# Five norms made as a row: two rounded products with a tile of 1/1024, root and reciprocal of the whole row

## The chip, the cores and the metric

The kernel runs on one core of one Trainium2 chip. The metric is the time on the device in microseconds (us), as the median of several runs.

## The reference

Two transformer blocks of width 1024 over 512 tokens, all in fp32. Cut to the order of work and the norms of the change:

```python
def rms_norm(x, w):                                    # over the 1024 channels of a token
    return x * rsqrt(mean(x * x, axis=-1) + 1e-6) * w

# first block
x = x + 0.5 * swiglu(rms_norm(x, norm_ffn1_w), w_in, w_out)        # n_ffn1
x = x + hybrid_mixer(rms_norm(x, norm_mix_w), ...)                 # n_mix
x = x + memory_cross_attention(rms_norm(x, norm_cross_w), ...)     # n_cross
x = x + 0.5 * swiglu(rms_norm(x, norm_ffn2_w), w_in, w_out)        # n_ffn2
x = rms_norm(x, norm_final_w)                                      # n_fin
# second block
...
x = x + rms_norm(mixed, g_post_mix)                                # n_post0, n_post1 (halves)
f = square(relu(rms_norm(x, g_pre_mlp) @ w_up)) @ w_down           # n_mlp
x = x + rms_norm(f, g_post_mlp)                                    # n_pmlp0, n_pmlp1 (halves)
x = x + sigmoid(rms_norm(x, g_ple) @ w_ple_gate) * (p @ w_proj)    # n_ple
```

## The kernel before

**Layout.** Activations lie transposed: channels on the 128 partitions in 8 chunks, the 512 tokens along a row. A weight unit is 128x1024 and gives one output tile of 128 channels by 512 tokens in 8 chunks. Every matrix product is made of three fp32r products (`products`, L510 on): rounded weight by rounded operand (L516), rounded weight by the operand's rest (L517), the weight's rest by the rounded operand (L518). The rounding is `w_hi` and `w_lo` for weights, `gx_hi` and `gx_lo` for the operand. A tile is 24 products.

**The stream of weights.** The 364 units go through a ring of four: SyncE loads `w_raw`, ScalarE casts it to `w_hi` (L1283), GpSimd subtracts to `w_lo` in four quarters (L463), TensorE uses it. ScalarE's casts stand in its program between its other work (`ahead`), three units ahead of use, and each waits until TensorE is done with the unit that had the slot.

**The norms.** The factor of a token isn't applied to the operand but to the result of the product, as a row `rstd_row` that all partitions hold (for instance L1851, which makes `ff_gate` from a bank and the row and thereby frees the bank). So TensorE starts on the first tiles of a stage before the factor is known, and it stops where all banks of the stage are full: `tiles` waits for `tile_free` of the bank's last use. The factor is made beside the first tiles, with two hooks that `norm_hooks` gives and that stand at fixed chunks in TensorE's stream:

1. `stat` (L700): the squares of the 8 chunks are already added up in `sumsq` (or `post_sum`, which is `rfin_row`). Four fp32 products of each 128 columns with a column of ones put the sums of 128 tokens each in a column of bank 7.
2. ScalarE takes the root of the 128x4 column with scale 1/1024 (L1296), VectorE its reciprocal (L1782).
3. `row` (L707): four transposes turn the column, broadcast over 128 partitions, into the 128x512 row in bank 7. VectorE copies it to `rstd_row` (L1786), and its next instruction uses it.

Where the hooks stand: in both feed-forward stages the first three tiles are made together; `stat` comes behind them, `row` behind chunk 3 of the fourth tile. For n_cross they stand behind the first tile of `cq` and behind chunk 3 of the second. For n_mlp they stand behind chunks 1 and 7 of a half tile in `tail_of_group`. For n_ple `stat` stands in `gate(3)`, and `row` between `project(0)` and `project(1)`; the second half of `project(1)` writes a bank that VectorE's first `gate` has to free.

**What sets the order.** All orders are written out by hand, one instruction stream for an engine, with semaphores between them. Each norm has a count on the semaphores `norm_stat`, `norm_root`, `norm_col`, `norm_row` and `norm_ready`, which `norm_count` computes.

## Time and profile before

| | |
|---|---|
| median of 3 runs | 2134.77 us (2134.74 to 2136.09) |
| span of the profiled execution | 2133.4 us |
| TensorE busy | 2114.8 us, 99% |
| VectorE, ScalarE, GpSimd busy | 829.8, 803.6, 1120.5 us |
| longest groups | the three products of `gx`, 675, 668 and 668 us |

The median of the runs is 1.4 us above the span, which runs from the first to the last instruction of the profiled execution. In the rows, PE is TensorE's products, PEld its weight loads, DVE VectorE, ACT ScalarE, POOL GpSimd. An arrow in brackets says who ended the idle time that stood before an instruction.

### The profile page before, as it was taken

What the parts mean: (1) busy time and instruction counts of PE and PEld (TensorE: products, weight loads), DVE (VectorE), ACT (ScalarE), POOL (GpSimd) and SP (SyncE); (2) the same over time, 40 slices, a digit from 0 to 9 for tenths busy, and PEclk for the clock granted to TensorE, in tenths of its full rate; (3) what the DMA queues carried; (4) which work ended last, traced back from release to release, by engine and by line L of the source; (5) the groups of instructions that cost most, each with busy time, mean ns of one, the idle gap of its engine ahead of it and who ended that gap; (6) DMA issues with size and microseconds to landing.
All of it is one profiled execution on the core that took longest, in us unless ns stands there. A gap on an engine that the chain in (4) does not pass through costs nothing.

```text
span 2133.4 us, 29164 instructions
## 1 busy us (share of the span) xinstructions
PE 2114.8 (99%) x10122; PEld 1740.7 (82%) x10122; DVE 829.8 (39%) x1489; ACT 803.6 (38%) x1345; POOL 1120.5 (53%) x1493
## 2 busy tenths in 40 slices
PE   9999999999999999999999999999999999999999
PEld 7888888878887778877888888887787888888887
DVE  5222211762841766143322222208744474023244
ACT  5222232325834655323322223326554343122233
POOL 6555555673354337725655555554545466555554
PEclk9999999999999999999999999999999999999999
DMA  6322233233322213412332223321222223332322
GB/s 214 119 98 98 99 106 106 85 99 96 114 99 79 75 55 122 155 40 89 99 98 98 95 94 117 99 96 63 79 89 79 89 80 108 99 99 99 99 89 80
DMA packets 61344, 207.71 MB, mean 97 GB/s; under 512 B 6616, under 2 KB 8088, under 8 KB 61256
## 3 DMA queue, kind: packets, MB, share of 16 engines
q1 hardware_dynamic: 55216, 195.84, 27.8%
q10 hardware_dynamic: 6040, 10.65, 1.5%
q8 instruction: 61, 1.00, 0.2%
q14 instruction: 27, 0.22, 0.0%
HBM read 204.31 MB, written 4.77 MB: 98 GB/s over the span
## 4 chain that ended last, share of the span: by engine, by line
PE 42%; issue 28%; POOL 27%; DVE 2%; POOLq 0%; ACT 0%; DMA 0%; SPq 0%; DVEq 0%; ACTq 0%
POOL w_lo L463 27%; PE bank L516 11%; PE bank L518 11%; PE bank L517 11%; PE bank L678 1%; PE bank L680 1%; PE bank L679 1%; PE bank L908 1%; PE bank L932 1%; PE bank L840 1%; PE bank L920 0%; DVE gx_lo L2394 0%; DVE bank L2403 0%; PE bank L846 0%; DVE x L2405 0%
## 5 line engine op out<-in xcount | busy, mean ns | idle before, releaser
L463 POOL TENSOR_TENSOR w_lo<-w_raw,w_hi 128x256 fp32r<-128x256 f32 x1448 | 1087.1, 783 | 933.4 <-ACT w_hi L1283 933.3
L516 PE MATMUL bank<-gx_hi,w_hi 128*128 128x512 f32 (+1 forms) x1768 | 674.9, 382 | 7.8 <-DVE gx_lo L2394 4.5
L518 PE MATMUL bank<-gx_hi,w_lo 128*128 128x512 f32 (+1 forms) x1768 | 668.1, 378 | 0.0
L517 PE MATMUL bank<-gx_lo,w_hi 128*128 128x512 f32 (+1 forms) x1768 | 667.6, 378 | 0.0
L1283 ACT CAST w_hi<-w_raw 128x1024 fp32r<-128x1024 f32 x364 | 378.4, 1045 | 347.9 <-PE bank L518 291.8
L516 PEld LDWEIGHTS bank<-gx_hi,w_hi 128*128 128x128 f32 x1768 | 332.6, 188 | 74.2 <-DVE gx_lo L2394 6.4
L518 PEld LDWEIGHTS bank<-gx_hi,w_lo 128*128 128x128 f32 x1768 | 332.5, 188 | 62.1
L517 PEld LDWEIGHTS bank<-gx_lo,w_hi 128*128 128x128 f32 x1768 | 332.7, 188 | 60.5 <-issue 0.2
L516 PE MATMUL bank<-ff_hi,w_hi 128*128 128x512 f32 x352 | 136.9, 389 | 0.0
L517 PE MATMUL bank<-ff_lo,w_hi 128*128 128x512 f32 x352 | 136.9, 389 | 0.0
L518 PE MATMUL bank<-ff_hi,w_lo 128*128 128x512 f32 x352 | 136.9, 389 | 0.0
L516 PE MATMUL bank<-up_hi,w_hi 128*128 128x512 f32 (+1 forms) x288 | 105.4, 366 | 0.0
L517 PE MATMUL bank<-up_lo,w_hi 128*128 128x512 f32 (+1 forms) x288 | 105.3, 365 | 0.0
L518 PE MATMUL bank<-up_hi,w_lo 128*128 128x512 f32 (+1 forms) x288 | 105.3, 365 | 0.0
L1854 DVE TENSOR_TENSOR ff_up<-bank,rstd_row 128x512 f32<-128x512 f32 x44 | 30.4, 690 | 189.9 <-PE bank L518 189.9
L1355 ACT CAST ff_hi<-ff_act 128x512 f32 (+1 forms) x44 | 27.3, 620 | 188.8 <-DVE ff_act L1858 188.8
L518 PEld LDWEIGHTS bank<-ff_hi,w_lo 128*128 128x128 f32 x352 | 66.1, 188 | 13.8
L516 PEld LDWEIGHTS bank<-ff_hi,w_hi 128*128 128x128 f32 x352 | 66.1, 188 | 13.7
L517 PEld LDWEIGHTS bank<-ff_lo,w_hi 128*128 128x128 f32 x352 | 66.1, 188 | 13.6
L1351 ACT ACTIVATE ff_silu<-ff_gate 128x512 f32<-128x512 f32 x44 | 27.8, 632 | 119.7 <-DVE ff_gate L1851 119.7
L1851 DVE TENSOR_TENSOR ff_gate<-bank,rstd_row 128x512 f32<-128x512 f32 x44 | 30.4, 691 | 90.7 <-PE bank L518 90.6
L678 PE MATMUL bank<-w_hi,gx_hi 128*128 128x512 f32 x160 | 63.7, 398 | 0.4 <-ACT z_tok L1337 0.4
(358 smaller groups left out, 2703.4 us busy)
## 6 DMA issues: line engine op xcount, KB each, us to landing
w_raw<-wstream SPq DMA_DIRECT2D x364, 512.0 KB, 3.5
bias_spread<-bias_rows ACTq DMA_DIRECT2D x1, 2560.0 KB
square<-cum_rows ACTq DMA_DIRECT2D x8, 256.0 KB, 3.5
rfin_row<-cum_rows ACTq DMA_DIRECT2D x8, 256.0 KB, 3.1
outT<-ple_o SPq DMA_DIRECT2D x8, 256.0 KB, 2.0
x<-xT SPq DMA_DIRECT2D x3, 512.0 KB, 8.0
square<-bias_spread ACTq DMA_DIRECT2D x4, 256.0 KB, 2.6
rfin_row<-bias_spread ACTq DMA_DIRECT2D x4, 256.0 KB, 2.7
```

The source lines that it names most:

```text
L463: ins = nc.gpsimd.tensor_tensor(w_lo[:, s, part], w_raw[:, s, part], w_hi[:, s, part].bitcast(F32), ALU.subtract)
L516: nc.tensor.matmul(dst, hi, rhs[0], start=first, stop=False)
L517: nc.tensor.matmul(dst, hi, rhs[1], start=False, stop=False)
L518: return nc.tensor.matmul(dst, lo, rhs[0], start=False, stop=last)
L678: nc.tensor.matmul(dst, a[0], rh, start=(k == 0), stop=False, skip_group_check=True)
L679: nc.tensor.matmul(dst, a[1], rh, start=False, stop=False, skip_group_check=True)
L680: mm = nc.tensor.matmul(dst, a[0], rl, start=False, stop=(k == DC - 1), skip_group_check=True)
L1283: nc.scalar.copy(w_hi[:, j, :], w_raw[:, j, :]).then_inc(unit_hi, 1)
L1351: nc.scalar.activation(ff_silu[:, :], ff_gate[:, :], ACT.Silu).then_inc(sem("ffn_silu"), 1)
L1355: nc.scalar.copy(tile_of(ff_hi, c), ff_act[:, :]).then_inc(sem("ffn_act_hi"), 1)
L1851: nc.vector.tensor_tensor(ff_gate[:, :], bank[2 * j][:, :], rstd_row[:, :], ALU.mult)\
L1854: nc.vector.tensor_tensor(ff_up[:, :], bank[2 * j + 1][:, :], rstd_row[:, :], ALU.mult)\
```

## The change

For n_ffn1, n_cross, n_ffn2, n_mlp and n_ple the column is gone. ScalarE rounds the sum row to `sum_hi` (`high_sum`), VectorE makes the rest `sum_lo` (`row_norm`), and one hook, `row_mean`, at the place of the old `row`, makes two fp32r products of 512 columns with a 128x128 tile `mean_r` of 1/1024. That sums over the partitions and puts the mean on all of them at once. ScalarE then takes the root of the 128x512 row from PSUM to `rstd_row` (`root_row`), and VectorE the reciprocal of that row in place. The other norms stay. The code for the new waits: ScalarE's two casts of weights now stand between `high_sum` and `root_row` in the feed-forward stages, one cast stands between them at n_cross, none at n_mlp, two at n_ple. `mean_r` is made once at the start, ahead of the small cast `wdt_hi`. Three tiles find their place in 15 KB that a smaller DMA scratch leaves; `x`, `cols` and `wdt` start 128 bytes lower, everything behind them where it was. Two semaphores for late loads become one, and `setup_hi` takes the place of `wdt_hi`.

```diff
+ROW_NORMS = ["n_ffn1", "n_cross", "n_ffn2", "n_mlp", "n_ple"]
...
+        sum_hi = fixed("sum_hi", [S], F32R)
+        sum_lo = fixed("sum_lo", [S], F32R)
+        mean_r = fixed("mean_r", [P], F32R)
+        assert cursor[0] <= 16384
+        cursor[0] = 16384
         x = fixed("x", [DC, S])
...
+            def row_mean(name):
+
+                def mean():
+                    if name == "n_ffn1":
+                        pe.wait_ge(sem("setup_hi"), 1)
+                    pe.wait_ge(norm_sem("col"), norm_count("col", name, 1))
+                    nc.tensor.matmul(bank[7][:, :], mean_r[:, :], sum_hi[:, :], start=True, stop=False)
+                    nc.tensor.matmul(bank[7][:, :], mean_r[:, :], sum_lo[:, :], start=False, stop=True)\
+                      .then_inc(norm_sem("row"), 1)
+                return mean
...
                 tiles(f"{name}_in", gx, DC, 4, peel=1, ready=gx_ready(before),
-                      hooks=norm_hooks(norm, before, together=3) + hooks, banks=4, together=3, opening=opening)
+                      hooks=(((3, 3), row_mean(norm)),) + hooks, banks=4, together=3, opening=opening)
...
-            (_, stat), (_, row) = norm_hooks("n_cross", "mix_attn")
-            one_tile("cq", 0, range(DC), gx, ready=gx_ready("mix_attn"), then={7: stat})
-            one_tile("cq", 1, range(DC), gx, then={3: row})
+            one_tile("cq", 0, range(DC), gx, ready=gx_ready("mix_attn"))
+            one_tile("cq", 1, range(DC), gx, then={3: row_mean("n_cross")})
...
-            (_, stat), (_, row) = norm_hooks("n_mlp", "post")
-            tail_of_group("up_a", {1: stat, 7: row})
+            tail_of_group("up_a", {7: row_mean("n_mlp")})
...
-            gate(3, {1: stat})
+            gate(3)
             project(0)
-            row()
+            row_mean("n_ple")()
             project(1)
...
+            def high_sum(name, summed):
+
+                if summed in POSTS:
+                    act.wait_ge(sem("post_summed"), post_count(summed, 2 * DC))
+                else:
+                    act.wait_ge(sem("summed"), sum_count(summed, DC + 1))
+                wait(act, norm_sem("row"), norm_count("row", name, 0))
+                nc.scalar.copy(sum_hi[:, :], (post_sum if summed in POSTS else sumsq)[:, :]).then_inc(sem("sum_hi"), 1)
+
+            def root_row(name):
+
+                act.wait_ge(norm_sem("row"), norm_count("row", name, 1))
+                nc.scalar.activation(rstd_row[:, :], bank[7][:, :], ACT.Sqrt, bias=eps_col[:, :], scale=1.0)\
+                  .then_inc(norm_sem("root"), 1)
...
                         if first(i) and j == 0:
-                            norm(norm_name)
+                            high_sum(norm_name, before)
                             for uu in (1, 2):
                                 ahead(f"{name}_in", i, 4, uu)
+                            root_row(norm_name)
...
+            nc.scalar.activation(mean_r[:, :], ones, ACT.Copy, scale=1.0 / D).then_inc(sem("setup_hi"), 1)
+            nc.scalar.copy(wdt_hi[:, :, :], wdt[:, :, :]).then_inc(sem("setup_hi"), 1)
...
+            def row_norm(name, summed):
+
+                src = post_sum if summed in POSTS else sumsq
+                if summed in POSTS:
+                    dve.wait_ge(sem("post_summed"), post_count(summed, 2 * DC))
+                dve.wait_ge(sem("sum_hi"), ROW_NORMS.index(name) + 1)
+                nc.vector.tensor_tensor(sum_lo[:, :], src[:, :], sum_hi[:, :].bitcast(F32), ALU.subtract)\
+                  .then_inc(norm_sem("col"), 1)
+                dve.wait_ge(norm_sem("root"), norm_count("root", name, 1))
+                nc.vector.reciprocal(rstd_row[:, :], rstd_row[:, :])\
+                  .then_inc(norm_sem("ready"), 1)
+                dve.wait_ge(norm_sem("ready"), norm_count("ready", name, 1))
...
-    nc = bacc.Bacc("TRN2", target_bir_lowering=False, num_devices=1)
+    nc = bacc.Bacc("TRN2", target_bir_lowering=False, num_devices=1, dynamic_dma_scratch_size=1024)
```

TensorE's rows at n_ffn2 before, from the last products of the third tile (bank 2) over the fourth (bank 3) to the row's block and beyond. `consts` holds the ones and the identity.

```order
L517 MATMUL bank2<-gx_lo_54,w_hi_56 128x512
L518 MATMUL bank2<-gx_hi_53,w_lo_57 128x512
L700 MATMUL bank7<-consts_58,sumsq_61 128x1 x4
L516 MATMUL bank3<-gx_hi_53,w_hi_56 128x512
...
L518 MATMUL bank3<-gx_hi_53,w_lo_57 128x512
L707 MATMUL bank7<-consts_58,rstd_col_70 128x128 x4
L516 MATMUL bank3<-gx_hi_53,w_hi_56 128x512
L517 MATMUL bank3<-gx_lo_54,w_hi_56 128x512
```

The same place of the change (L524 to L526 are the three products there):

```order
L525 MATMUL bank2<-gx_lo_57,w_hi_59 128x512
L526 MATMUL bank2<-gx_hi_56,w_lo_60 128x512
L524 MATMUL bank3<-gx_hi_56,w_hi_59 128x512
...
L526 MATMUL bank3<-gx_hi_56,w_lo_60 128x512
L726 MATMUL bank7<-sum_hi_49,mean_r_51 128x512
L727 MATMUL bank7<-sum_lo_50,mean_r_51 128x512
L524 MATMUL bank3<-gx_hi_56,w_hi_59 128x512
```

The block behind the third tile is gone, and the block behind twelve products of the fourth is two products of 512 columns.

ScalarE's rows at the same norm before, from the end of stage `co` on:

```order
L1308 ACTIVATE square<-x 128x512
L1283 CAST w_hi<-w_raw 128x1024
L1296 ACT_TABLE_LOAD
L1296 ACTIVATE root_col<-bank,eps_col 128x4
L1283 CAST w_hi<-w_raw 128x1024 x2
L1351 ACT_TABLE_LOAD
L1351 ACTIVATE ff_silu<-ff_gate 128x512
```

And of the change:

```order
L1334 ACTIVATE square<-x 128x512
L1294 CAST w_hi<-w_raw 128x1024
L1311 CAST sum_hi<-sumsq 128x512
L1294 CAST w_hi<-w_raw 128x1024 x2
L1316 ACT_TABLE_LOAD
L1316 ACTIVATE rstd_row<-bank,eps_col 128x512
L1378 ACT_TABLE_LOAD
L1378 ACTIVATE ff_silu<-ff_gate 128x512
```

The root stands behind the two casts of weights now, and the cast of the sum ahead of them.

## Rows read from the trace of the kernel before

**Rows 1.** The page: its first line and part 1, busy time of each engine.

```profile
span 2133.4 us, 29164 instructions
...
PE 2114.8 (99%) x10122; PEld 1740.7 (82%) x10122; DVE 829.8 (39%) x1489; ACT 803.6 (38%) x1345; POOL 1120.5 (53%) x1493
```

**Rows 2.** Timeline of TensorE around n_ffn2: start us, us, instruction.

```profile
1015.60 0.95 PE L700 MATMUL bank<-consts,sumsq 128*128 128x1 f32 x8
...
1016.72 0.39 PE L517 MATMUL bank<-gx_lo,w_hi 128*128 128x512 f32 x1
...
1019.22 0.60 PE L707 MATMUL bank<-consts,rstd_col 128*128 128x128 f32 x4
...
1022.40 0.39 PE L516 MATMUL bank<-gx_hi,w_hi 128*128 128x512 f32 x1
```

**Rows 3.** The waits of TensorE: us in total, times, longest.

```profile
PE bank L516 <- POOL w_lo L463: 2.3, 3, 1.1
```

**Rows 4.** Timeline around n_ffn2, of ScalarE and of VectorE.

```profile
1016.58 0.26 ACT L1296 ACTIVATE root_col<-bank,eps_col 128x4 f32<-128x4 f32 x1 [12.97 <-PE bank L700]
...
1019.85 0.69 DVE L1786 COPY rstd_row<-bank 128x512 f32<-128x512 f32 x1 [2.80 <-PE bank L707]
1020.58 0.69 DVE L1851 TENSOR_TENSOR ff_gate<-bank,rstd_row 128x512 f32<-128x512 f32 x1
```

**Rows 5.** Groups of ScalarE by shape: us in total, mean ns of one.

```profile
L1643 ACT ACTIVATE stick_w<-bank 128x512 f32<-128x512 f32 x16 | 8.7, 603 | 0.8 <-PE bank L1148 0.8
...
L1337 ACT ACTIVATE z_tok<-bank,rstd_col 128x512 f32<-128x512 f32 x8 | 4.8, 688 | 6.0 <-PE bank L680 6.0
```

**Rows 6.** Groups of VectorE by shape, three sizes of reciprocal.

```profile
L1782 DVE RECIPROCAL rstd_col<-root_col 128x4 f32<-128x4 f32 x6 | 1.1, 178 | 57.4 <-ACT root_col L1296 57.4
...
L2049 DVE RECIPROCAL xrec<-xsum 128x16 f32<-128x16 f32 x1 | 0.3, 254 | 2.2 <-ACT xsum L1479 2.2
...
L2237 DVE RECIPROCAL fin<-fin 128x8 f32<-128x8 f32 x1 | 0.2, 202 | 0.8 <-ACT fin L1599 0.8
```

**Rows 7.** Timeline of TensorE around n_cross.

```profile
887.10 0.60 PE L707 MATMUL bank<-consts,rstd_col 128*128 128x128 f32 x4
...
890.28 0.39 PE L516 MATMUL bank<-gx_hi,w_hi 128*128 128x512 f32 x1
```

**Rows 8.** Timeline around n_mlp: ScalarE, TensorE, GpSimd, VectorE.

```profile
1733.88 2.94 ACT L1283 CAST w_hi<-w_raw 128x1024 fp32r<-128x1024 f32 x3 [2.08 <-PE bank L518]
...
1758.26 1.05 ACT L1283 CAST w_hi<-w_raw 128x1024 fp32r<-128x1024 f32 x1
...
1738.47 0.60 PE L707 MATMUL bank<-consts,rstd_col 128*128 128x128 f32 x4
...
1735.00 12.99 POOL L463 TENSOR_TENSOR w_lo<-w_raw,w_hi 128x256 fp32r<-128x256 f32 x16 [2.39 <-ACT w_hi L1283]
...
1742.54 1.17 DVE L2451 TENSOR_TENSOR up_lo<-up_a,up_hi 128x512 fp32r<-128x512 f32 x1 [0.69 <-ACT up_hi L1724]
```

**Rows 9.** Timeline around n_ple, of TensorE and of VectorE.

```profile
2098.51 0.60 PE L707 MATMUL bank<-consts,rstd_col 128*128 128x128 f32 x4
...
2100.11 0.40 PE L518 MATMUL bank<-p_hi,w_lo 128*128 128x512 f32 x1
2100.62 0.50 PE L516 MATMUL bank<-p_hi,w_hi 128*128 128x512 f32 x1
...
2099.88 1.29 DVE L2498 TENSOR_TENSOR ple_t<-bank,rstd_row 128x512 f32<-128x512 f32 x2
```

**Rows 10.** Timeline around n_ffn1: ScalarE, GpSimd, TensorE.

```profile
19.62 0.28 ACT L1393 CAST wdt_hi<-wdt 128x128 fp32r<-128x128 f32 x1
...
20.94 4.67 POOL L463 TENSOR_TENSOR w_lo<-w_raw,w_hi 128x256 fp32r<-128x256 f32 x4 [3.10 <-ACT w_hi L1283]
...
25.73 0.95 PE L700 MATMUL bank<-consts,sumsq 128*128 128x1 f32 x8
...
33.79 0.50 PE L516 MATMUL bank<-gx_hi,w_hi 128*128 128x512 f32 x1
```

More of the change, by code:

```diff
@@ L115, in norm_count @@
             n = NORMS.index(name)
+            if step == "stat":
+                n -= sum(m in ROW_NORMS for m in NORMS[:n])
             if step == "ready":
@@ L1215, in _ @@
             group_by_halves("ple2a", "pmlp", {(0, 3): stat1, (0, 5): row1}, second=4)
-            (_, stat), (_, row) = norm_hooks("n_ple", "pmlp")
             pe.wait_ge(sem("p_lo"), 2)
@@ L1338, in token_evac, with ffn @@
                                          scale=scale[:, t:t + 1]).then_inc(sem("token_free"), 1)
-            def ffn(name, norm_name, weight, out_peel=0):
+            def ffn(name, norm_name, before, weight):
                 def block_of(i):
@@ L1392, in _ @@
             act.wait_ge(sem("setup_in"), 16 * 3)
-            nc.scalar.copy(wdt_hi[:, :, :], wdt[:, :, :]).then_inc(sem("wdt_hi"), 1)
+            nc.scalar.activation(mean_r[:, :], ones, ACT.Copy, scale=1.0 / D).then_inc(sem("setup_hi"), 1)
+            nc.scalar.copy(wdt_hi[:, :, :], wdt[:, :, :]).then_inc(sem("setup_hi"), 1)
             def spread_bias():
@@ L1401, in spread_bias @@
                    .then_inc(sem("bias_spread"), 16)
-            ffn("ffn1", "n_ffn1", "norm_mix_w")
+            ffn("ffn1", "n_ffn1", "load", "norm_mix_w")
             def xbc(x_part):
@@ L1574, in _ @@
             ahead("cq", 0, 4, 0)
-            norm("n_cross")
+            high_sum("n_cross", "mix_attn")
             ahead("cq", 0, 4, 1)
+            root_row("n_cross")
             ahead("cq", 0, 4, 2)
@@ L1592, in _ @@
             residual_stage("co", "norm_ffn2_w", 1)
-            ffn("ffn2", "n_ffn2", None)
+            ffn("ffn2", "n_ffn2", "co", None)
             ahead("qk2", 0, 4, 0)
@@ L1721, in block_of @@
                         if first(i) and j == 0 and half == 0:
-                            norm("n_mlp")
+                            high_sum("n_mlp", "post")
+                            root_row("n_mlp")
                         act.wait_ge(sem("up_act"), half * HC + c + 1)
@@ L1755, in _ @@
             ahead("ple2a", 0, 4, 1)
-            norm("n_ple")
+            high_sum("n_ple", "pmlp")
             ahead("ple2a", 0, 4, 2)
             ahead("ple2a", 0, 4, 3)
+            root_row("n_ple")
             ahead("ple2a", 0, 4, 4)
@@ L1841, in scaled_tiles, with ffn @@
                 blocks(dve, count // body, block_of)
-            def ffn(name, norm_name, weight):
+            def ffn(name, norm_name, before, weight):
                 def block_of(i):
@@ L1848, in block_of @@
                         if first(i) and j == 0:
-                            norm(norm_name)
+                            row_norm(norm_name, before)
                         dve.wait_ge(unit_done, U + 1)
@@ L1916, in bias_rows @@
                   .then_inc(sem("brow_ready"), 1)
-            dve.wait_ge(sem("wdt_hi"), 1)
+            dve.wait_ge(sem("setup_hi"), 2)
             nc.vector.tensor_tensor(wdt_lo[:, :, :], wdt[:, :, :], wdt_hi[:, :, :].bitcast(F32), ALU.subtract)\
               .then_inc(sem("wdt_lo"), 1)
-            ffn("ffn1", "n_ffn1", "norm_mix_w")
+            ffn("ffn1", "n_ffn1", "load", "norm_mix_w")
             nc.vector.memset(conv_in[:, 0:3], 0.0).then_inc(sem("conv_pad"), 1)
@@ L2197, in _ @@
             scaled_tiles("ck", kx_T, 8, row=m_row)
-            norm("n_cross")
+            row_norm("n_cross", "mix_attn")
             def scale_q(c):
@@ L2227, in _ @@
             residual_stage("co", "norm_ffn2_w", 1, 1.0, "n_ffn2")
-            ffn("ffn2", "n_ffn2", None)
+            ffn("ffn2", "n_ffn2", "co", None)
             dve.wait_ge(norm_sem("root"), norm_count("root", "n_fin", 1))
@@ L2441, in block_of @@
                         if first(i) and j == 0 and half == 0:
-                            norm("n_mlp")
+                            row_norm("n_mlp", "post")
                         dve.wait_ge(unit_done, UNIT0[stage] + c + 1)
@@ L2493, in _ @@
             down_post(*range(6, 16))
-            norm("n_ple")
+            row_norm("n_ple", "pmlp")
             def gate(m):
```

19 lines of the change are left out of this document (7 added, 12 removed).

## The prediction

> **What bounds the kernel now.** I read the page first. TensorE is busy 99% of the span of 2133.4 us, the other engines 38 to 53% [rows 1], so a microsecond counts where TensorE issues less or waits. Then I went by time through the five norms of the change, on TensorE, VectorE and ScalarE. A fp32r product of 512 columns starts every 0.227 us: the eleven from 1016.72 to 1019.22 take 2.50 us [rows 2]. All of TensorE's waits for a weight's low half sum to 2.3 us [rows 3], so little waiting stands behind the norms that could take up a delay.
>
> At a norm the products run on while the row of factors is made. The first VectorE instruction that uses the row also empties the bank that TensorE wants some products later. What matters is when that instruction starts, against when TensorE arrives.
>
> **What TensorE saves.** Before, a norm put two blocks into the stream of products: four fp32 products of one column (L700) and four transposes (L707). From L700 at 1015.60 to L707 at 1019.22 are 3.62 us, and the twelve products between are 2.72: the first block costs 0.90. From L707 to the first product of the next tile at 1022.40 are 3.18 us, again with twelve products: the second costs 0.46 [rows 2]. Both are gone, two fp32r products of 512 columns come (2 x 0.227 = 0.45). That saves 0.91 us at each of five norms, 4.5 us in all, if nothing waits.
>
> **What the row takes.** Counted from the start t of the row's block.
> - Before: t = 1019.22, and the first user of the row, ff_gate, starts at 1020.58 [rows 2, 4]: t + 1.36.
> - After, the second product starts at t + 0.23 and ends 0.39 later (the duration of a product [rows 2]), t + 0.62. ScalarE starts 0.03 later, as it did behind L700 (1015.60 + 0.95 = 1016.55, start 1016.58 [rows 2, 4]).
> - The root of 512 elements from PSUM: an ACTIVATE of that size is 0.603 us without a column operand (stick_w) and 0.688 with one as its scale (z_tok) [rows 5]. The root has one as its bias; I take 0.68: t + 1.33.
> - The reciprocal of 512 elements in place, which no row shows. Its small forms do: 178 ns for 4 elements, 202 for 8, 254 for 16 [rows 6]. That is 6.0 and 6.5 ns an element, on 0.154 fixed. A copy of 512 is 0.69 us [rows 4], about 1.05 ns an element. So the bounds are 0.69 us (if wide rows ran like a copy) and, from the steepest pair, 0.25 + 496 x 6.5 ns = 3.48 us. Three sizes lie on one line, so I take 0.154 + 512 x 6.26 ns = 3.36 us, near the upper end.
> - With 0.03 on each side, the first user starts at t + 4.78, 3.4 us later behind its block than before. From there to TensorE's next product are 0.74 us (2099.88 to 2100.62 [rows 9]).
>
> The Trainium skill ("VectorE: DVE Perf Modes", the walkthrough of the 8-slice pipeline) says that Reciprocal is an iterative divide with a repeat count of 8. Eight cycles of 1.05 ns would make 4.45 us, 1.1 us more at each place that waits; the slope of the rows is nearer to six, so the sum goes by the rows.
>
> **Place by place.** t moves 0.90 us ahead everywhere, as the first block is gone.
> - n_ffn2: t = 1018.32, ff_gate at 1023.10, TensorE's tile 4 at 1023.84. Before it was 1022.40: **+1.44**. TensorE arrives at 1021.49 and stands 2.35 us. Behind ff_gate on VectorE stand ff_up, ff_act and ff_lo, and with them ScalarE's cast of a later weight; tile 5 needs ff_up 0.7 us later, while a tile is 5.45 us, so nothing more waits. The sum's high half (ScalarE) and low half (VectorE) cost nothing: ScalarE idles there for 13 us [rows 4] under running products, and VectorE waits for it. The table load for the root stands behind the two weight casts and ahead of the wait, as before.
> - n_cross: t = 887.10 - 0.90 = 886.20, the first scaled tile of q starts at 890.98, the product that wants its bank at 891.72, before 890.28 [rows 7]: **+1.44**.
> - n_ffn1: here the first block hid that the fourth weight's low half is ready only at 20.94 + 4.67 = 25.61, beside 25.73 when the products reach L700. The new tile of 1/1024 is made on ScalarE ahead of that weight's cast; it is as wide as the small cast at 19.62, 0.28 us [rows 10], of which I count 0.19, since neighbours there overlap. Ready at 25.80, start 25.85: 0.12 lost. t = 25.85 + 2.72 = 28.57, product at 34.09, before 33.79: **+0.30**. It is small since two narrow products (L724, L725) stand between and gave a slack of their own.
> - n_mlp: ScalarE's three casts end at 1736.82, only then comes the sum's high half (0.6 us, 1737.4), then the low half on VectorE, 0.69 us free or 1.17 us while GpSimd splits weights beside it, as it does from 1735.0 to 1748.0 [rows 4, 8]: 1738.1 to 1738.6. TensorE would be there at 1738.47 - 0.90 = 1737.57. This is a wait that the change adds: 0.5 to 1.1 us against 0.91 saved, -0.4 to +0.2; GpSimd is busy, so +0.1. Bank pressure isn't there (two other banks come first, 11 us), but VectorE's tiles run 3.6 us late. The cast at 1758.26 waits behind them; late it ends at 1762.9, its four splits of 0.81 us at 1766.15. TensorE wants that weight at 1738.93 + 5 x 24 x 0.227 = 1766.17 [rows 8]. The slack of 3.6 us is just used up; I add 0.1: **+0.2**.
> - n_ple: t = 2098.51 - 0.90 = 2097.61, ple_t at 2102.39, the product that waits for it at 2103.13, before 2100.62 [rows 9]: **+2.51**. Here TensorE waited for the row already (a product at 2100.11, the next not at 2100.34 but at 2100.62), so nothing of the 0.91 is kept and the whole delay goes to the end, with all results behind it.
>
> Sum: 1.44 + 1.44 + 0.30 + 0.2 + 2.51 = **+5.9 us**. The profiled execution has a span of 2133.4 us [rows 1], so 2139.3; the median of the runs lies 1.4 above the span, which gives **2140.7 us**, +0.28%. The x tile and two small ones move by 128 bytes, the rest of the memory stays, and no DMA is added or moved past a queue: nothing for these.
>
> **The rivals.**
> 1. *The reciprocal of a wide row runs like a copy*, 0.69 us. For it: the rows have no form over 16 elements. Against: their even slope. Then the products would reach n_cross and n_ffn2 unhindered (-0.91 each), n_ffn1 -0.79, n_mlp +0.1, n_ple 2100.46 against 2100.62, -0.16: -2.7 us, **2132.1**. This is the case on the other side. It decides from a reciprocal under 1.8 us on; under about 2.95 us the loss falls below 0.2%. Chance 0.09 with all that lies between.
> 2. *Each element takes eight cycles*: +1.1 us at four places and as much late at n_mlp, where the slack is gone: **2145 to 2146**. Chance 0.09. This is what the rule of the Trainium skill named above would bring.
> 3. *Part of the delays is given back*: the waits of rows 3, the freer VectorE after n_mlp (its slow forms of 1.17 us lie in GpSimd's work, which would be past), and at n_mlp the uncontended 0.69. That would take 1.5 to 3 us off: **2137.5 to 2139**. Against: the waits are small and follow TensorE's own products. Chance 0.15.
> 4. *TensorE's saving alone counts*, -4.5 us, 2130.2: only if every row came in time, which n_ple excludes even with the copy. 0.02.
>
> **Chances and range.** My forecast 0.65, with its own range 2139 to 2142.5 (0.1 us of reciprocal is 0.4 us of the sum, 0.1 of the root another 0.4, n_mlp 0.6). 0.2% is 4.3 us here, about what the measurement tells from no change: the line is at 2139.0. Slower by more: the forecast but for a tail of 0.03, rival 2, a little of 3 and of what I don't see, together 0.75. Within: most of rival 3 (0.11), that tail and most of rival 1 (0.07), 0.21. Faster: the rest of rival 1 and rival 4, 0.04. The range that holds 8 in 10 reaches over rival 3 below and to the near edge of rival 2 above: 2137 to 2145.5.
>
> **What the new profile would show.** The reciprocal of 128x512 at 3.3 to 3.5 us, the root at 0.68, the two new products 0.227 apart. Gaps on TensorE ended by ff_gate of about 1.1 us (n_ffn1) and 2.35 (n_ffn2), by qx_T of 2.35 at n_cross; at n_mlp one of 0.5 to 1.1 ended by the low half of the sum; at n_ple some 3.7 us ended by ple_t. Wrong I am above all if the reciprocal isn't 3.4 us, counted four times; next, if a later weight or bank takes up or adds to the delay.

## The result, and the profile after

| | before | after |
|---|---|---|
| median of 5 runs, one after the other | 2134.74 us (2133.87 to 2136.09) | 2147.47 us (2145.08 to 2148.16) |
| ratio of the runs, 95% interval | | 1.0057 [1.0046, 1.0067] |
| span of the profiled execution | 2133.4 us | 2145.7 us |
| mean granted TensorE clock | 1.000 | 0.997 |

The changed kernel is 0.57% slower. The sign of the prediction was right, its size was not: +5.9 us were forecast, +12.3 us came (2145.7 - 2133.4), and the median of 2147.47 lies outside the range of 2137 to 2145.5.

The page of the changed kernel, its first line and part 1, beside [rows 1]:

```profile
span 2145.7 us, 29076 instructions
...
PE 2117.4 (99%) x10072; PEld 1740.3 (81%) x10072; DVE 850.5 (40%) x1489; ACT 808.5 (38%) x1351; POOL 1120.1 (52%) x1493
```

TensorE has 50 products less and is still busy 2.6 us longer. Single products must have become slower somewhere.

Groups of the changed kernel by shape (line, engine, operation, count | us in total, mean ns of one | idle before), for the reciprocal and the low half of the sum:

```profile
L1829 DVE RECIPROCAL rstd_row<-rstd_row 128x512 f32<-128x512 f32 x5 | 16.8, 3353 | 28.0 <-ACT rstd_row L1316 28.0
...
L1826 DVE TENSOR_TENSOR sum_lo<-sumsq,sum_hi 128x512 fp32r<-128x512 f32 x3 | 9.3, 3107 | 25.3 <-ACT sum_hi L1311 25.3
```

The reciprocal takes 3.353 us (3.36 forecast). The subtraction that makes sum_lo takes 3.1 us in the mean of three (0.69, 0.69 and 7.94): an average over unlike members asks for their single rows.

The waits of TensorE in the changed kernel (us in total, times, longest), those that the change touches:

```profile
PE bank L524 <- DVE ple_t L2542: 3.5, 1, 3.5
PE bank L524 <- DVE ff_gate L1895: 3.4, 2, 2.3
...
PE bank L726 <- DVE sum_lo L1826: 3.3, 2, 2.6
PE bank L524 <- POOL w_lo L471: 2.3, 3, 1.1
...
PE bank L524 <- DVE qx_T L2246: 0.7, 1, 0.7
```

The two waits for ff_gate and the one for ple_t were forecast (1.1 and 2.35, 3.7). The wait of 2.6 us for sum_lo was not: it is at n_cross, where the forecast had 2.35 us for qx_T.

### n_cross

Timelines of the changed kernel around n_cross: VectorE, then GpSimd.

```profile
880.73 7.94 DVE L1826 TENSOR_TENSOR sum_lo<-sumsq,sum_hi 128x512 fp32r<-128x512 f32 x1 [24.60 <-ACT sum_hi L1311]
890.28 3.35 DVE L1829 RECIPROCAL rstd_row<-rstd_row 128x512 f32<-128x512 f32 x1 [1.61 <-ACT rstd_row L1316]
...
849.82 38.31 POOL L471 TENSOR_TENSOR w_lo<-w_raw,w_hi 128x256 fp32r<-128x256 f32 x55
```

The subtraction lasts 7.94 us, from 880.73 to 888.67. GpSimd's row is part of one unbroken run of splits, here from 849.82 to 888.13 (55 splits): no idle time stands in it, and during the subtraction a split starts every 0.68 to 0.70 us. The subtraction ends 0.54 us after that run.

The kernel before has a gap in GpSimd's run at this place. GpSimd, then ScalarE, before:

```profile
837.56 47.44 POOL L463 TENSOR_TENSOR w_lo<-w_raw,w_hi 128x256 fp32r<-128x256 f32 x68 [1.61 <-ACT w_hi L1283]
885.74 2.82 POOL L463 TENSOR_TENSOR w_lo<-w_raw,w_hi 128x256 fp32r<-128x256 f32 x4 [0.74 <-ACT w_hi L1283]
...
884.62 1.04 ACT L1283 CAST w_hi<-w_raw 128x1024 fp32r<-128x1024 f32 x1
```

GpSimd, then ScalarE, in the changed kernel:

```profile
837.98 50.14 POOL L471 TENSOR_TENSOR w_lo<-w_raw,w_hi 128x256 fp32r<-128x256 f32 x72 [1.60 <-ACT w_hi L1294]
...
883.50 1.05 ACT L1294 CAST w_hi<-w_raw 128x1024 fp32r<-128x1024 f32 x1 [2.80 <-PE bank L526]
```

Before, the cast stood behind the root and came at 884.62, so GpSimd idled from 885.00 to 885.74. In the change it stands ahead of the root and comes at 883.50, and GpSimd goes on without a gap, 72 splits in place of 68. So the order of ScalarE's casts has its part in the long operation.

The same operation inside a run of splits at n_mlp, and that run, in the changed kernel:

```profile
1745.58 0.94 DVE L1826 TENSOR_TENSOR sum_lo<-rfin_row,sum_hi 128x512 fp32r<-128x512 f32 x1 [5.42 <-ACT sum_hi L1311]
...
1743.13 8.83 POOL L471 TENSOR_TENSOR w_lo<-w_raw,w_hi 128x256 fp32r<-128x256 f32 x12 [2.37 <-ACT w_hi L1294]
```

Here it took 0.94 us, though the run goes on for 5.4 us behind it. So a run of splits alone doesn't hold a subtraction up until its end. In this trace 80 TENSOR_TENSOR operations with two SBUF operands begin while GpSimd works with its next operation right behind. In 77 of them one GpSimd operation ended before they did, in 2 two, and in the one at n_cross eleven.

TensorE at n_cross, in the changed kernel:

```profile
888.73 0.50 PE L726 MATMUL bank<-sum_hi,mean_r 128*128 128x512 f32 x1 [2.59 <-DVE sum_lo L1826]
889.06 0.46 PE L727 MATMUL bank<-sum_lo,mean_r 128*128 128x512 f32 x1
889.32 0.63 PE L524 MATMUL bank<-gx_hi,w_hi 128*128 128x512 f32 x1
889.74 0.63 PE L525 MATMUL bank<-gx_lo,w_hi 128*128 128x512 f32 x1
...
892.94 0.39 PE L524 MATMUL bank<-gx_hi,w_hi 128*128 128x512 f32 x1
893.17 0.40 PE L525 MATMUL bank<-gx_lo,w_hi 128*128 128x512 f32 x1
...
894.50 0.47 PE L524 MATMUL bank<-gx_hi,w_hi 128*128 128x512 f32 x1 [0.70 <-DVE qx_T L2246]
```

It stands 2.59 us at L726. Then, from 889.32 on, products start 0.43 us apart where they start 0.23 apart again from 892.94 on.

### The granted clock

Stretches of the changed kernel (busy time and count of PE, PEld, DVE, ACT and POOL, then PEclk, the granted clock as a share of 2.4 GHz, DMA share, GB/s): behind the stand at n_cross; in and behind that at n_ffn2; among the small waits of the post norm; in and behind that at n_ple.

```profile
888.70:893.00 4.30, 4.28 (x12) 3.38 (x13) 2.72 (x1) 0.69 (x1) 0.00 (x0) 0.60 0.36 122
1025.00:1028.00 3.00, 0.98 (x5) 0.48 (x3) 2.97 (x2) 0.30 (x1) 0.56 (x1) 1.00 0.59 194
1029.30:1032.50 3.20, 3.20 (x9) 2.51 (x8) 2.41 (x5) 1.61 (x3) 0.00 (x0) 0.50 0.00 0
...
1722.20:1725.40 3.20, 3.20 (x17) 3.20 (x17) 1.65 (x4) 1.08 (x3) 2.91 (x6) 0.50 0.15 35
...
2107.90:2111.00 3.10, 0.00 (x0) 0.00 (x0) 3.06 (x2) 1.49 (x2) 2.77 (x4) 1.00 0.42 155
2111.40:2114.50 3.10, 3.10 (x8) 2.42 (x9) 2.93 (x5) 2.09 (x3) 0.94 (x2) 0.50 0.57 191
```

TensorE stands at full clock, and when it goes on, some 3 us of its work run at 0.50, which is 1.2 GHz: PE looks fully busy there, with 8 or 9 products of 512 columns where some 14 fit (3.2 / 0.227; the 17 at 1722 are narrower ones). So the page's busy time grew. There are four such stretches; in the profiled execution of the kernel before there was none until 2131.

### Where the 12.3 us came in

The start of the same product in both traces gives the delay as it grows. At the three big norms it stands in rows: 890.28 against 894.50, +4.22 [rows 7]; 1022.40 against 1028.24, +5.84 [rows 2]; 2100.62 against 2111.34, +10.72 [rows 9]. The rows of the changed kernel for n_ffn2 and n_ple:

```profile
1028.24 0.49 PE L524 MATMUL bank<-gx_hi,w_hi 128*128 128x512 f32 x1 [2.26 <-DVE ff_gate L1895]
...
2111.34 0.80 PE L524 MATMUL bank<-p_hi,w_hi 128*128 128x512 f32 x1 [3.54 <-DVE ple_t L2542]
```

Taken over all products, with the saving of 0.9 us a norm inside each site's number:

| place | forecast | measured | of it unforeseen |
|---|---|---|---|
| n_ffn1 | +0.30 | +0.39 | |
| the stretch 842 to 853, small waits | 0 | -0.51 | given back |
| n_cross | +1.44 | +4.34 | wait for sum_lo 2.6, low clock some 1.5 |
| n_ffn2 | +1.44 | +1.41 | |
| behind it, low clock | 0 | +1.72 | 1.7 |
| post norm, 1715 to 1723 | 0 | +0.3 to 0.4 | low clock |
| n_mlp | +0.2 | +0.1 | |
| n_ple | +2.51 | +2.42 | |
| behind it, low clock | 0 | +1.53 | 1.5 |

The rows sum to about 11.8 us; the rest of the 12.3 is spread over steps under 0.3 us. Of the 6.4 us that came beyond the forecast (12.3 - 5.9), low clock at three norms is 4.7, and what the late subtraction adds at n_cross is 1.4 (4.34 - 1.44 - 1.5).

### The profile page after: what moved, and what is told of

It reads as the page before. It is cut to its first block, busy times and chain, and to the rows that moved or that the text cites. A ratio compares the mean times of both kernels' runs of the same rounds, so it can differ in the third digit from the quotient of the medians.

```text
span 2145.7 us, 29076 instructions
## 1 busy us (share of the span) xinstructions
PE 2117.4 (99%) x10072; PEld 1740.3 (81%) x10072; DVE 850.5 (40%) x1489; ACT 808.5 (38%) x1351; POOL 1120.1 (52%) x1493
## 4 chain that ended last, share of the span: by engine, by line
PE 41%; issue 28%; POOL 27%; DVE 2%; ACT 0%; POOLq 0%; DMA 0%; SPq 0%; DVEq 0%; ACTq 0%
POOL w_lo L471 27%; PE bank L524 11%; PE bank L526 10%; PE bank L525 10%; PE bank L686 1%; PE bank L688 1%; PE bank L687 1%; PE bank L922 1%; PE bank L946 1%; PE bank L854 1%; PE bank L934 0%; DVE gx_lo L2438 0%; DVE bank L2447 0%; DVE x L2449 0%; PE bank L860 0%
## 5 line engine op out<-in xcount | busy, mean ns | idle before, releaser
L524 PE MATMUL bank<-gx_hi,w_hi 128*128 128x512 f32 (+1 forms) x1768 | 676.5, 383 | 10.9 <-DVE ff_gate L1895 3.4
L526 PE MATMUL bank<-gx_hi,w_lo 128*128 128x512 f32 (+1 forms) x1768 | 669.7, 379 | 0.0
L524 PEld LDWEIGHTS bank<-gx_hi,w_hi 128*128 128x128 f32 x1768 | 334.0, 189 | 78.5 <-issue 9.6
L526 PEld LDWEIGHTS bank<-gx_hi,w_lo 128*128 128x128 f32 x1768 | 334.0, 189 | 63.1
L524 PE MATMUL bank<-ff_hi,w_hi 128*128 128x512 f32 x352 | 136.9, 389 | 0.0
L526 PE MATMUL bank<-ff_hi,w_lo 128*128 128x512 f32 x352 | 136.9, 389 | 0.0
L524 PE MATMUL bank<-up_hi,w_hi 128*128 128x512 f32 (+1 forms) x288 | 105.4, 366 | 0.0
L526 PE MATMUL bank<-up_hi,w_lo 128*128 128x512 f32 (+1 forms) x288 | 105.2, 365 | 0.0
L526 PEld LDWEIGHTS bank<-ff_hi,w_lo 128*128 128x128 f32 x352 | 66.1, 188 | 13.7
L524 PEld LDWEIGHTS bank<-ff_hi,w_hi 128*128 128x128 f32 x352 | 66.1, 188 | 13.6
```

The lines of the kernel that those rows point to most:

```text
L524: nc.tensor.matmul(dst, hi, rhs[0], start=first, stop=False)
L526: return nc.tensor.matmul(dst, lo, rhs[0], start=False, stop=last)
```

## The experiments

Three groups of kernels ran, each on one chip beside the kernel before: e1 to e4 (2135.14 us there), r_after, e5, e6 and p_probe (2135.44), q_probe, e7 and e8 (2135.40). Theory A: the reciprocal, the long subtraction at n_cross and the low clock behind stands make the loss. Its rivals are named with each run.

### e1_copy: the reciprocal's price

A copy in place stands for the reciprocal, so the factor that the tiles are scaled with is the root and not its inverse: that part of the computation is left out.

```diff
-                nc.vector.reciprocal(rstd_row[:, :], rstd_row[:, :])\
+                nc.vector.tensor_copy(rstd_row[:, :], rstd_row[:, :])\
```

> The change with one edit: the reciprocal of the row is a plain copy in place (the factor is then the root and not its reciprocal, so that part of the computation is left out). Theory A (the reciprocal of 3.35 us is what the products wait for at n_cross, n_ffn2 and n_ple, and the granted clock falls to its lower level after each wait of over two microseconds): the waits at n_ffn2 (2.26 us) and n_ple (3.54) shrink to nothing or under 1 us, no half-clock spell there; only the wait for the low half of the sum at n_cross (2.6 us) and the spell behind it stay. 12.7 us of loss less 2.67 at n_cross is not all recovered there; in all 2134 to 2137 us. Rival B (the row's way through ScalarE and the two products is what is late, the reciprocal only part of it): more than 2 us of waits stay at n_ffn2 and n_ple, 2140 us or more.

Measured: 2135.7 us, ratio 1.0001 [0.9992, 1.0011]. No stretch of low clock is left in the profiled execution (2134.88 us); two of the other nine, of 2137.1 and 2137.4 us, show a mean clock of 0.998. The long subtraction stays. VectorE at n_cross in e1_copy:

```profile
880.40 7.37 DVE L1826 TENSOR_TENSOR sum_lo<-sumsq,sum_hi 128x512 fp32r<-128x512 f32 x1 [24.61 <-ACT sum_hi L1311]
889.30 0.43 DVE L1829 COPY rstd_row<-rstd_row 128x512 f32<-128x512 f32 x1 [1.54 <-ACT rstd_row L1316]
```

The reciprocal decides 11.8 us (2147.5 - 2135.7), though it adds only 2.9 us (3.35 - 0.43) at each of five places and TensorE hides some of that. The changed kernel's stands for ff_gate and ple_t are 6.9 us; the difference is more than that. The low clock behind the stands would fill it, which this run alone doesn't show.

### e2_psum: the subtraction from a bank

At n_cross ScalarE also copies the sum into the norm's bank, and VectorE subtracts from there. One of its two operands is then in PSUM.

```diff
+                if name == "n_cross":
+                    nc.scalar.copy(bank[7][:, :], sumsq[:, :])
...
-                src = post_sum if summed in POSTS else sumsq
+                src = bank[7] if name == "n_cross" else post_sum if summed in POSTS else sumsq
```

> The change with one edit at n_cross: ScalarE also copies the sum into bank 7, and VectorE subtracts the high half from that copy, so that this instruction has one operand in SBUF and one in PSUM in place of two in SBUF. Theory A (VectorE's subtraction of two SBUF operands stood 7.94 us because GpSimd's splits, back to back until 888.1, kept it out): it takes 0.7 us, no wait ahead of the new products at n_cross, the wait for the bank behind them grows to 2.3 us, and with the clock's fall still there the time is 1 to 1.5 us less, 2146. Rival B (it was late or slow for its own reasons, as the cast before it or the place of the new tiles): it stays at several microseconds and the time stays at 2147.5.

Measured: 2145.87 us, ratio 1.0046 [1.0029, 1.0063]. VectorE at n_cross in e2_psum, under an unbroken run of splits on GpSimd:

```profile
884.17 0.69 DVE L1828 TENSOR_TENSOR sum_lo<-bank,sum_hi 128x512 fp32r<-128x512 f32 x1 [25.13 <-ACT sum_hi L1313]
```

7.94 us became 0.69. The time fell by 1.6 us alone, because TensorE now stands for qx_T instead (2.3 us), as the forecast had it. Low clock came at three places (behind the stands at n_ffn1 and n_cross, and in the post norm), and not the stands of 2.3 us at n_ffn2 and 3.5 us at n_ple: it doesn't follow every stand.

### e3_fill: TensorE kept busy in the stands

e2_psum with products that nothing reads: 9 each in the stands at n_cross and n_ffn2, 14 at n_ple.

```diff
+            def fill(b, count):
+                for _ in range(count):
+                    nc.tensor.matmul(bank[b][:, :], mean_r[:, :], sum_hi[:, :], start=True, stop=True)
```

> The kernel of e2_psum with products that nothing reads where TensorE waits for a bank: 9 at n_cross, 9 at n_ffn2 (2.04 us each time) and 14 at n_ple (3.2 us). Theory A (TensorE's granted clock falls to half for 3.41 us after it has stood for over two microseconds, and each spell costs 1.5 to 1.7 us): no half-clock spell behind the three norms, and the time is 4 to 5 us less than e2_psum, about 2141.5, though no wait got shorter. Rival B (the spells come from elsewhere or cost nothing, as the products behind them have slack): the time is that of e2_psum or more, by up to the products added.

Measured: 2143.01 us, ratio 1.0034 [1.0023, 1.0046], 2.9 us under e2_psum. The one stretch of low clock left is behind the stand at n_ffn1 (34.3 to 37.8), which is not filled. More work on TensorE made the kernel faster. But e2_psum had none at two of the filled places either, so this run alone doesn't show what filling does there; e7_stand and e8_busy do.

### e4_early: the same work, asked for earlier

e2_psum, with the products of the mean earlier in TensorE's stream (6 products earlier at n_ffn1, 12 at n_ffn2 and n_cross, 18 at n_ple), and the root ahead of one weight cast on ScalarE.

```diff
-                      hooks=(((3, 3), row_mean(norm)),) + hooks, ...
+                      hooks=((((3, 1) if norm == "n_ffn1" else (2, 7)), row_mean(norm)),) + hooks, ...
...
-            one_tile("cq", 0, range(DC), gx, ready=gx_ready("mix_attn"))
-            one_tile("cq", 1, range(DC), gx, then={3: row_mean("n_cross")})
+            one_tile("cq", 0, range(DC), gx, ready=gx_ready("mix_attn"), then={7: row_mean("n_cross")})
+            one_tile("cq", 1, range(DC), gx)
...
-            gate(3)
+            gate(3, {5: row_mean("n_ple")})
             project(0)
-            row_mean("n_ple")()
```

> The kernel of e2_psum with the row's products earlier: at n_ffn1 two chunks earlier, at n_ffn2 right behind the third tile, at n_cross behind the first tile, at n_ple in the half tile before; and on ScalarE the root ahead of one of the weight casts that stood before it. Theory A (the change costs only what TensorE stands, and the row's longer way of 3.4 us can lie under products if it starts 12 products earlier): the waits at n_cross, n_ffn2 and n_ple go, no half-clock spell, and the saving of 0.91 us at each norm shows: 2130 to 2132 us, less than the kernel before. Rival B (the sum isn't ready so early, or ScalarE's casts and table load hold the root back, or the weights come late): one or more waits of a microsecond stay, 2133 to 2138.

Measured: **2132.02 us, ratio 0.9984 [0.9974, 0.9993]**, under the kernel before and 15.5 us under the changed one, with the same operations and a copy more. No low clock, and of the five norms only n_mlp waits. From e4_early's waits of TensorE:

```profile
PE bank L726 <- DVE sum_lo L1827: 0.7, 1, 0.7
```

So the row is not too dear at these places, it was asked for too late; what the bank at n_cross adds to that, e6_sbuf tells.

### e5_mlp: the last wait

The rounding of the sum at n_mlp moves ahead of ScalarE's third weight cast.

```diff
-            for uu in (1, 2, 3):
+            for uu in (1, 2):
                 ahead("up_a", 0, 4, uu)
+            high_sum("n_mlp", "post")
+            ahead("up_a", 0, 4, 3)
```

> e4_early with the rounding of the sum at n_mlp one weight cast earlier on ScalarE. In e4_early TensorE still stands 0.7 us for sum_lo at n_mlp. If ScalarE's order is what makes that sum late, the stand goes and the kernel takes 2131.0 to 2131.8 us (0.3 to 1.0 us under e4_early's 2132.0). Rival: the post norm's last row is what is late, and the sum waits for it; then the stand stays at 0.7 us and the time at 2132.0 +- 0.4, or the delayed cast costs up to 0.7 us.

Measured: 2132.03 us, ratio 0.9984 [0.9975, 0.9993], no gain that can be seen, where 0.3 to 1.0 us were expected. The wait for sum_lo fell from 0.7 to 0.2 us, so ScalarE's order was its cause; in this execution 0.4 us of wait for ff_gate came back at n_ffn1.

### e6_sbuf: e4_early without the bank

Both operands of the subtraction come from SBUF again, all else is e4_early.

```diff
-                if name == "n_cross":
-                    nc.scalar.copy(bank[7][:, :], sumsq[:, :])
...
-                src = bank[7] if name == "n_cross" else post_sum if summed in POSTS else sumsq
+                src = post_sum if summed in POSTS else sumsq
```

> e4_early, but at n_cross the sum is not copied into a bank: the subtraction reads both operands from SBUF again, as in the changed kernel, while the products that need it now stand 5 us earlier, behind tile 0. Theory A (a VectorE operation that reads two SBUF operands gets nothing done while GpSimd's splits run back to back): it starts at about 880.7 us and ends only where GpSimd's stream breaks off, 3 to 8 us later, so TensorE stands 1.5 to 6 us at its product (e4_early: none over 0.2 us there), and the kernel takes 2134 to 2140 us. Rival (the bank copy did nothing, the earlier place alone repaired n_cross): the subtraction takes about 0.7 us, no stand, 2131.5 to 2132.5 us.

Measured: 2134.37 us, ratio 0.9996 [0.9987, 1.0006], 2.35 us over e4_early (2.05 if each is taken against its own group's kernel before). VectorE, GpSimd and ScalarE at n_cross in e6_sbuf:

```profile
880.53 4.57 DVE L1825 TENSOR_TENSOR sum_lo<-sumsq,sum_hi 128x512 fp32r<-128x512 f32 x1 [24.61 <-ACT sum_hi L1310]
...
854.53 30.03 POOL L471 TENSOR_TENSOR w_lo<-w_raw,w_hi 128x256 fp32r<-128x256 f32 x43
...
885.93 0.69 ACT L1315 ACTIVATE rstd_row<-bank,eps_col 128x512 f32<-128x512 f32 x1 [5.43 <-PE bank L727]
886.52 1.05 ACT L1293 CAST w_hi<-w_raw 128x1024 fp32r<-128x1024 f32 x1
```

GpSimd's run ends at 884.56, the subtraction at 885.10, again 0.54 later. That the run ends 3.6 us sooner than in the changed kernel goes with ScalarE's order: here the root stands ahead of the next cast of weights, the root waits for the products with sum_lo, and the cast comes only at 886.52, behind it. GpSimd has no weights from 884.56 on, and its idle time lets the subtraction through: the long operation is released by the stand that it causes itself. In the changed kernel one more cast stood ahead of the root, and the next one behind it. This is read from the rows; the order of the casts wasn't tried apart.

### p_probe and q_probe: which operations are held up

e4_early, with two operations more on VectorE at 855 us, where it idles and GpSimd's splits run back to back. Their results are used by nothing.

```diff
+            link(nc.vector.tensor_scalar(sum_lo[:, :], sumsq[:, :], 2.0, None, ALU.mult))
+            link(nc.vector.tensor_tensor(sum_lo[:, :], sumsq[:, :], sumsq[:, :], ALU.add))
```

> e4_early with two additional operations on VectorE ahead of n_cross, where GpSimd's splits run back to back and VectorE is idle: first sum_lo <- sumsq * 2 (one SBUF operand), then sum_lo <- sumsq + sumsq (two SBUF operands); their values are overwritten by the norm and used by nothing. Theory A: the first takes 0.4 to 0.8 us, the second many us, up to the whole stretch until GpSimd's stream breaks off; the time is 0 to 5 us over e4_early, by how long it blocks VectorE. Rival (any VectorE operation on SBUF is held up there, by the writes or by traffic of the DMA queues): both take several us. Rival (only the third read of a same tile or the particular tiles matter): both take under 1.3 us.

VectorE in p_probe, then GpSimd:

```profile
855.21 29.00 DVE L2243 TENSOR_SCALAR sum_lo<-sumsq 128x512 fp32r<-128x512 f32 x1
884.24 0.69 DVE L2244 TENSOR_TENSOR sum_lo<-sumsq 128x512 fp32r<-128x512 f32 x1
...
854.60 29.33 POOL L471 TENSOR_TENSOR w_lo<-w_raw,w_hi 128x256 fp32r<-128x256 f32 x42
```

I was wrong here: the operation with one SBUF operand was held up for 29.0 us, until 0.28 us behind GpSimd's run. One execution gave 2139.01 us. The second probe has in its place a reciprocal, which is slow by itself:

```diff
-            link(nc.vector.tensor_scalar(sum_lo[:, :], sumsq[:, :], 2.0, None, ALU.mult))
+            link(nc.vector.reciprocal(rstd_row[:, :], sumsq[:, :]))
```

> The measured 29.0 us of tensor_scalar with one SBUF operand refutes the theory that two SBUF operands are what holds VectorE up. Two theories stand. B: what is held up is any operation that moves more than the plain rate allows from or to SBUF, that is, one with two SBUF operands, and one that runs at two elements a cycle (the copy of 512 elements took 0.43 us, the tensor_scalar would too); the reciprocal, at 6.25 ns an element and one SBUF operand, is not held up. C: every VectorE operation from SBUF to SBUF is held up. The kernel is p_probe with a reciprocal (rstd_row <- sumsq, a value used by nothing) in place of the tensor_scalar, at the same place at 855 us, and the two-operand addition behind it. B: the reciprocal takes 3.35 us, from 855.2 to 858.6, and the addition behind it about 25 us, until GpSimd's stream breaks off near 884. C: the reciprocal takes about 32 us, until 887, and the addition 0.7 us.

VectorE in q_probe, then GpSimd (one execution, 2138.85 us):

```profile
855.48 3.35 DVE L2243 RECIPROCAL rstd_row<-sumsq 128x512 f32<-128x512 f32 x1
858.86 26.46 DVE L2244 TENSOR_TENSOR sum_lo<-sumsq 128x512 fp32r<-128x512 f32 x1
...
854.83 29.94 POOL L471 TENSOR_TENSOR w_lo<-w_raw,w_hi 128x256 fp32r<-128x256 f32 x43
```

The reciprocal ran its 3.35 us beside GpSimd as if alone, and the addition of two SBUF operands was held up for 26.5 us. What was held up here is an operation with two SBUF operands and a tensor_scalar from SBUF to SBUF. The second kind is, by e1_copy's copy of 512 elements in 0.43 us against the 0.69 of rows that read a bank [rows 4], one that runs at double rate; the tensor_scalar's own time wasn't measured. The Trainium skill ("SBUF — State Buffer", section "SBUF: two separate sides") gives just these two kinds as those that contend with GpSimd for a port pair shared under an exclusive lock, held for the whole of one instruction; these runs agree on the kinds. They differ from the wait of one instruction that this lets expect: in p_probe 42 splits went by, each a single instruction.

Why the subtraction was passed over at n_cross and served after one split elsewhere is open. One difference stands in the traces: GpSimd had made over 20 splits without a pause when the held-up operations began (since 837.98 in the changed kernel, since 836.49 in p_probe), and in the changed kernel at most some 9 undisturbed ones ahead of any other operation of these kinds. No run tried that apart.

### r_after: the changed kernel once more

No edit.

> The changed kernel once more, word for word, in another execution. Theory A (the reciprocal's 3.35 us, the starved subtraction at n_cross, and spells of half clock behind some stands): 2145 to 2149 us; the subtraction sum_lo<-sumsq,sum_hi at n_cross takes 6 to 9 us again, because GpSimd's stream of splits stands at the same place in the program; the stands of TensorE at the five norms are the same to 0.3 us (1.1, 2.6, 2.3, 0.7, 3.5). The spells of 1.2 GHz are the part that may move: two to four of them, each of 3.41 us, each starting within 2 us behind a stand of 1 us or more, but not behind every such stand. Rival (the spells belong to fixed places of the program): exactly the four places of the first trace. Rival (the starved subtraction was an accident of one execution): it takes 0.7 to 1.3 us here.

Measured: 2147.61 us, ratio 1.0057 [1.0042, 1.0073]. The subtraction at n_cross took 7.37 us. TensorE's stands were 1.7 and 2.3 (ff_gate), 2.0 (sum_lo at n_cross) and 3.5 us (ple_t), so two of them moved by 0.6 where 0.3 was expected. Low clock came with those at n_ffn1, n_cross and n_ple, with the last for 6.8 us and from 0.7 us before TensorE went on, and not the one at n_ffn2, nor did the post norm show it. Stretches of r_after at n_ffn1, n_cross, n_ffn2 and n_ple:

```profile
34.60:37.90 3.30, 3.30 (x8) 2.63 (x9) 2.51 (x5) 1.17 (x3) 0.00 (x0) 0.50 0.32 123
...
891.40:894.60 3.20, 3.20 (x9) 2.48 (x8) 3.00 (x1) 0.16 (x1) 0.00 (x0) 0.50 0.33 124
1027.00:1033.00 6.00, 3.75 (x17) 2.86 (x16) 5.18 (x7) 1.42 (x3) 0.00 (x0) 1.00 0.29 94
2109.90:2116.60 6.70, 6.07 (x14) 4.78 (x15) 6.40 (x10) 4.09 (x6) 2.41 (x4) 0.50 0.45 158
```

The waits belong to the program, the low clock comes with some of them, others in each execution. The sum was alike in both: four times 3.4 us at half clock in the first trace, 3.4, 3.4 and 6.8 us here.

### e7_stand and e8_busy: the price of a stand, with and without work in it

e7_stand is e4_early with two more reciprocals of 256 elements at n_ffn2 and at n_ple; e8_busy is e7_stand with 12 products that nothing reads in each of the two stands.

```diff
+                if name in ("n_ffn2", "n_ple"):
+                    for _ in range(2):
+                        link(nc.vector.reciprocal(rstd_row[:, 0:256], rstd_row[:, 0:256]))
```

> e4_early, which has no spell of half clock and no stand over 0.5 us at these places, with two more reciprocals of 256 elements (1.7 us each; the second undoes the first) ahead of the one at n_ffn2 and at n_ple, so that TensorE stands 2.5 to 3.5 us at each. Theory A: the stands alone add 5 to 7 us, and each that is followed by a spell of 1.2 GHz adds 1.4 to 1.7 us more: 2137 to 2142 us, with none, one or two spells. Rival (the spells in the earlier runs came from something else in the changed kernel): no spell, 2137 to 2139 us.

```diff
-            ffn("ffn2", "n_ffn2", "co")
+            ffn("ffn2", "n_ffn2", "co", hooks=(((3, 7), lambda: fill(5, 12)),))
...
+                    if m == 3:
+                        pe.wait_ge(norm_sem("root"), norm_count("root", "n_ple", 1))
+                        fill(7, 12)
```

> e7_stand with 12 products whose results are used by nothing in each of the two stands (2.7 us of work in each). If a stand of TensorE is what the spells follow, no spell follows here, and the kernel takes 2137 to 2139.5 us, under e7_stand by what its spells cost (0 to 3.4 us). Rival (spells do not hang on the stands): as many spells as e7_stand, and the same time, or up to 0.5 us more where the filling outlasts the stand.

Measured: e7_stand 2143.69 us, ratio 1.0038 [1.0024, 1.0053]; e8_busy 2139.18 us, ratio 1.0017 [1.0007, 1.0027]; e4_early 2132.02. The stretches behind n_ffn2 and behind n_ple, of e7_stand:

```profile
1023.50:1029.50 6.00, 6.00 (x14) 4.72 (x15) 4.35 (x7) 3.88 (x6) 1.14 (x2) 0.50 0.00 0
...
2108.20:2111.40 3.20, 3.20 (x9) 2.46 (x8) 3.13 (x5) 1.45 (x2) 1.67 (x2) 0.50 0.55 211
```

The same two of e8_busy:

```profile
1023.50:1029.50 6.00, 6.00 (x27) 4.96 (x28) 4.34 (x7) 3.88 (x6) 1.12 (x2) 1.00 0.00 0
...
2108.20:2111.40 3.20, 3.20 (x15) 2.63 (x14) 3.01 (x6) 2.11 (x3) 1.51 (x2) 1.00 0.26 99
```

In both kernels TensorE goes on at the same moment at n_ffn2, 1023.44 and 1023.45. In e7_stand, which stood idle for 3.72 us until then, 14 products ran in the next 6 us; in e8_busy, which had worked, 27. The delays alone cost 7.2 us (2139.18 - 2132.02); left idle they cost 4.5 us more (2143.69 - 2139.18). In the two traces that difference grows only inside the stretches at half clock. It isn't one execution's accident: nine of e8_busy's ten executions have a mean clock of 1.000 and one 0.999, e7_stand's five have 0.996 to 0.998. This pair shows that for stands of 3.7 us the low clock hangs on the stand being idle, and its price.

## Why the prediction was wrong

- **What TensorE saves**, 0.91 us a norm: right. in the changed trace the delay falls by 0.9 where the first block stood at n_cross (882.6), before any stand. e4_early is 3.4 us under before in its span, against 4.5 for five savings; n_mlp, where it waits for sum_lo, gives 0.9 of them back.
- **The row's times**: right. The root took 0.69 us (0.68), the reciprocal 3.353 (3.36), the products start 0.227 us apart. Three small sizes gave a wide operation's time within 0.2%. That the law is a straight line was the insight; the last digit is luck, since their two slopes of 6.0 and 6.5 ns allowed 3.2 to 3.5 us.
- **n_ffn2, n_ple, n_ffn1, n_mlp**: right, within 0.1 us each (table above). At n_mlp the stand was 0.69 us, for sum_lo, as forecast.
- **n_cross failed.** The step said of the sum's halves that they "cost nothing" and "VectorE waits for it", worked out at n_ffn2, where it holds, and carried to n_cross in silence. The low half took 7.94 us there in place of 0.69, and TensorE stood 2.59 us for it. I had a row of that kind in hand, an operation of two SBUF operands at 1.17 us beside GpSimd's splits [rows 8], took it for a surcharge of 0.5 us, and applied it at n_mlp alone. At n_mlp that held (0.94 us); at n_cross the operation waited for the end of GpSimd's run. GpSimd's timeline of before would have told only half of it: its run ends at 885.00, and a subtraction let through there would end at about 885.5 (an estimate: 0.54 later, as in the runs), ahead of t = 886.20. That the new order of ScalarE closes this gap had to be seen too. Price: 2.9 us of the miss (4.34 - 1.44), of which 1.4 are the late subtraction and 1.5 low clock; with the operand in a bank (e2_psum) the forecast wait for qx_T came, 2.3 us.
- **A term was missing, and it is the largest part of the miss: the granted clock.** The forecast put stands of 1.1, 2.35, 2.35 and 3.7 us into a stream whose longest was 1.6 us, and counted them at their length. Some were followed by work at 1.2 GHz. Three such stretches cost 1.5, 1.7 and 1.5 us, 4.7 in all. e7_stand against e8_busy shows for stands of 3.7 us that they hang on the idle stand; for those of 2.3 and 2.6 us it is argued from their place. Why the clock fell at the post norm too is open. The Trainium skill ("TensorE: Matmul & The Clock Gate", section "HAM oscillation — how this bites in real kernels") describes waits that throw TensorE back to the low clock in each round of a loop. I had not weighed it; the traces agree for some of the stands, not for all.
- **The rivals.** The first (a reciprocal like a copy, 2132.1) named the right lever: e1_copy gave 2135.7, with a stand of 2.0 us for the long subtraction, which that rival hadn't either. The second (eight cycles an element) would have come near the measured time for a wrong reason: the reciprocal has 6.25 ns an element and a fixed part. The third was there with 0.5 us, not 1.5 to 3.
- **Open**: which stand is followed by low clock. At n_ffn2 the same stand of 2.3 us was followed by it in the changed kernel's first trace and not in its second, the one of 3.5 us at n_ple in both, but not in e2_psum. The post norm shows low clock in some traces (the first of the changed kernel, e2_psum, both probes) and not in others, with waits of about 1 us there in all of them; and q_probe has a stretch at 0.50 from 1369.1 to 1372.5 with no stand ahead of it. The kernel before isn't free of low clock either: of its 14 executions beside e7_stand, the two slowest, 2136.47 and 2137.98 us, have a mean clock of 0.998 and 0.997. What decides it wasn't tried apart. Open too is why the subtraction was passed over at n_cross alone (p_probe and q_probe).

## What to carry to other kernels

Where a fixed latency grows on a side engine, first try to ask for it earlier: the same row cost 12.7 us (2147.47 - 2134.74) at its place in the change and gained 3.1 (2135.14 - 2132.02) where it was asked for 6 to 18 products sooner at four norms, with one operand in a bank at n_cross; without the bank (e6_sbuf) it gained 1.1 (2135.44 - 2134.37), which the interval doesn't tell from nothing. Allow for a stand of TensorE costing more than its length (11.7 us for 7.4 us of stands in e7_stand), unless other products fill it; some stands cost only their length. Before a VectorE operation with two SBUF operands (or a copy from SBUF to SBUF) goes on the path, look at GpSimd's timeline there, with the change's own order of casts. If a long run without a gap stands there, put one operand into a bank: it needn't be held up, but at n_cross it was in every trace that had it so.
